# Level scores of a gated recurrence: one product of 128 rows with both heads side by side, or one product of 64 rows for each head

## The chip, the cores and the metric

The kernel is one program on 1 core of a Trainium2 chip. The metric is the device time of an execution in microseconds (us); the time before is a median of 3 runs. Everything is 32-bit float. An f32 product appears in the trace as two records of TensorE work (PE) and two weight loads (PEld); one such record is called a pass here.

## What is computed

One inference step of a backbone of two layers for 1024 latent and 128 context tokens. The change lies in one of the three mixers of a layer, the bidirectional gated linear recurrence with 4 heads of width 64:

```python
def step(state, blk):
    qc, kc, vc, gc = blk
    b = jnp.cumsum(gc, axis=2)
    o_inter = jnp.einsum('nhtk,nhkv->nhtv', qc * jnp.exp(b), state)
    rel = jnp.where(lower, b[:, :, :, None, :] - b[:, :, None, :, :], -jnp.inf)
    att = jnp.einsum('nhtk,nhtsk,nhsk->nhts', qc, jnp.exp(rel), kc)
    o = o_inter + jnp.einsum('nhts,nhsv->nhtv', att, vc)
...
o, s_fin = _gla_chunk_scan(
    jnp.concatenate([q, rev(q)], axis=0),
    jnp.concatenate([k_f, rev(k_b)], axis=0),
    jnp.concatenate([v, rev(v)], axis=0),
    jnp.concatenate([g_f, rev(g_b)], axis=0),
    s0.reshape(2 * B, HG_HEADS, HG_DK, HG_DV))
```

Within a chunk, `att` holds for each query t and each earlier key s the sum over k of q·exp(b_t − b_s)·k. The kernel works on chunks of 128 tokens (NT = 9 of them: 8 latent, 1 context).

## The kernel before

`project_and_recur` is one stage of a layer. On TensorE it does the input projection (`piece()`, 8 products of 128x128 weights each, lines L288 with 256 columns and L291 with 384) and, threaded between the pieces, the recurrence. Two heads share a tile of 128 partitions: head 0 of a pair `ct` lies on partitions 0 to 63, head 1 on 64 to 127.

To avoid overflow in exp(b_t − b_s), the scores are made in levels: at level h a chunk is cut into blocks of 2h tokens, and the queries of one half of each block meet the keys of the other half, with weights relative to the middle of the block. There are 7 levels (h = 64 ... 1) for each of two directions, and two "plain" steps for the diagonal, which take both gates' keys and so twice the products: 16 steps for a pair of heads, NS = 32 steps in a layer, in the order `seq`. Only half of the tokens are queries at a level, 64 of each chunk.

A step n passes three engines:

- VectorE (DVE), in the order `span(n + 2)`, `operands(n + 1)`, `place(n)`. `span` takes two differences (L647, L648). `operands` makes the weighted keys (L665) and the weighted queries in two operations, one for each head's 64 partitions (L668, twice). `place` copies the scores of both heads from PSUM under a mask into `att` (L685).
- ScalarE (ACT): the exponential of the weights (L512), or for a plain step a copy of the queries in two operations (L519). It also empties the pieces' PSUM banks (L433).
- TensorE: `level_scores(n)`. For each chunk the weights are the keys (128 partitions, 128 tokens), and the moving operand is `xq`, 128 partitions by 2 x 64 columns. Head 0's queries stand in the first 64 columns on partitions 0 to 63, head 1's in the last 64 columns on partitions 64 to 127; the rest of `xq` was cleared once by GpSimd (POOL), so that one product gives both heads' scores (L336, 9 products, 18 passes; 36 passes in a plain step).

Scores of even and odd steps lie in two regions of 1536 columns (three PSUM banks of 512) each. A `piece()` follows the scores of 26 of the 32 steps (`with_piece`); steps 3, 7, 11, 19, 23 and 27 are followed directly by the next step's scores. Up to step 9 the pieces are of 384 columns, from step 10 on of 256. After steps 15 and 31 comes `recurrent_out` (L348, L352). After the last step the stage goes on with projection pieces to its end. TensorE's order is written out:

```python
for n in range(NS):
    level_scores(n)
    if n in with_piece:
        piece()
    if n in (NS // 2 - 1, NS - 1):
        recurrent_out(n // (NS // 2))
```

Other lines that come up below: L315 (`state_updates`) are products on 64 columns of the array, L706 the chain of states on DVE ahead of step 0; L812 are the score products of the attention stage, on rows 0 to 63 and 64 to 127 of the array in turn, each pair into two banks; L826 are transposes, L1137 products of 64 rows in the filter stage, and L1201 plain products of 128 rows and 512 columns.

Of the kernel before, what the change touches and what calls it, by code (L numbers as in the profile page):

```python
# [19 lines left out]
ALU = mybir.AluOpType  # L20
ACT = mybir.ActivationFunctionType
AX = mybir.AxisListType

P = 128
# [3 lines left out]
TOK = LAT + CTX  # L28
NT = TOK // P
# [6 lines left out]
DQ = 64  # L36
# [10 lines left out]
LEVELS = [64, 32, 16, 8, 4, 2, 1]  # L47
# [78 lines left out]
def project_and_recur(nc, m, l):  # L126
# [8 lines left out]
                "keys_taken", "decay", "update", "chained", "s_stored", "s_cleared", "mask_loaded", "att_cleared",  # L135
                "span", "cleared", "weight", "operand", "plain", "scores", "placed", "out_done", "out_taken", "g_loaded",
                "step", "root", "out_ready", "hg_turned", "hg_kept")
# [37 lines left out]

    def queries(b, hh, h):
        return m.xq[hh * DQ:(hh + 1) * DQ, b, :, hh].rearrange("p c (b j) -> p c b j", j=h)

# [4 lines left out]
    with stage(nc, m, *HG_NAMES, *PR_NAMES, *AT_NAMES) as (block, s):  # L183
# [72 lines left out]
        @block.gpsimd  # L256
        def _(pool):
            for d in range(2):
                last = nc.gpsimd.memset(m.S[d][:, :, :, :], 0.0)
            last.then_inc(s["s_cleared"], 1)  # L260
            nc.gpsimd.memset(m.xq[:, :, :, :, :], 0.0)
            pool.wait_ge(s["transposed"], 4)
            nc.gpsimd.memset(m.X[:, :, :], 0.0).then_inc(s["cleared"], 1)
            pool.wait_ge(s["update"], len(steps))
            for ct in range(2):
                nc.gpsimd.memset(m.att[:, ct], 0.0).then_inc(s["att_cleared"], 1)
            pool.wait_ge(s["tables_loaded"], 32)
            for i in range(8):
                pool.wait_ge(s["shuffled"], i + 1)
                x = m.aqk[:, i, 0:LAT]  # L270
                nc.gpsimd.tensor_tensor(x, x, m.cos[:, :], ALU.mult).then_inc(s["kept"], 1)

        @block.tensor
        def _(pe):
# [45 lines left out]
            def level_scores(n):  # L320
                ct, d, lev = seq[n]
                if n == 0:
                    pe.wait_ge(s["chained"], 8 * len(steps))
                if n >= 2:
                    pe.wait_ge(s["placed"], n - 1)
                if n == NL + len(LEVELS):
                    pe.wait_ge(s["out_taken"], 3)
                if lev < len(LEVELS):
                    pe.wait_ge(s["operand"], ops[n])
                else:  # L330
                    pe.wait_ge(s["plain"], n + 1 - ops[n])
                operands = [m.X[:, n % 2]] if lev < len(LEVELS) else [m.fk[:, ct], m.fk[:, 2 + ct]]
                for ch in range(NT):
                    at = (n % 2) * 1536 + ch * P
                    for keys in operands:
                        last = nc.tensor.matmul(m.ps[:, at:at + P], keys[:, ch * P:(ch + 1) * P],  # L336
                                                m.xq[:, n % 2, ch].rearrange("p hh t -> p (hh t)"),
                                                start=keys is operands[0], stop=keys is operands[-1])
                last.then_inc(s["scores"], 1)

            def recurrent_out(ct):
                pe.wait_ge(s["placed"], (ct + 1) * (NS // 2))
                for ch in range(NT):
                    at = ch * P
# [5 lines left out]
                    for hh in range(2):  # L350
                        h = 2 * ct + hh
                        last = nc.tensor.matmul(m.ps[:, at + hh * DQ:at + (hh + 1) * DQ], m.att[:, ct, hh, ch, :],  # L352
                                                m.hi[:, ch, h * DQ:(h + 1) * DQ], start=(ch == LT),
                                                stop=(hh == 1 or ch == LT))
# [44 lines left out]
        def _(act):  # L399
# [106 lines left out]
            def weight(n):  # L506
# [7 lines left out]
                else:  # L514

                    act.wait_ge(s["scores"], n - 1)
                    for hh in range(2):
                        r = slice(hh * DQ, (hh + 1) * DQ)
                        last = nc.scalar.activation(  # L519
                            m.xq[r, n % 2, :, hh],  # L520
                            m.hq[r, ct].rearrange("p (c j two) -> p c j two", c=NT, two=2)[:, :, :, lev - len(LEVELS)],
                            ACT.Copy)
                    last.then_inc(s["plain"], 1)

# [42 lines left out]
        def _(dve):  # L567
# [82 lines left out]
            def operands(n):  # L650
# [14 lines left out]
                nc.vector.tensor_tensor(keys, wk, k0, ALU.mult)  # L665
                for hh in range(2):
                    r = slice(hh * DQ, (hh + 1) * DQ)
                    last = nc.vector.tensor_tensor(queries(b, hh, h), wq[r], q0[r], ALU.mult)  # L668
                last.then_inc(s["operand"], 1)

            def place(n):
# [4 lines left out]
                else:  # L676
                    dve.wait_ge(s["placed"], n)
                h = LEVELS[lev] if lev < len(LEVELS) else 1
                dat = m.ps[:, (n % 2) * 1536:(n % 2) * 1536 + TOK]\
                    .rearrange("p (c hh b j) -> p hh c b j", c=NT, hh=2, j=h)  # L680
                msk = m.mask[:, d, lev].rearrange("p (b j) -> p b j", j=h)
# [1711 lines left out]
def build(nc, d, outs):  # L2393
    m = Mem()
# [3 lines left out]
    with ExitStack() as ctx:  # L2398
# [39 lines left out]
        m.E = view(38692, 2, TOK)  # L2438
        m.xq = view(40996, 2, NT, 2, 64)
        m.ke_t = view(43300, NT, 4, P)  # L2440
# [245 lines left out]
```

## Time and profile before

| | us |
|---|---|
| median of 3 runs (lowest, highest) | 4122.88 (4119.47, 4123.29) |
| the profiled execution's own time | 4124.99 |
| its span, first to last instruction | 4123.2 |
| PE busy | 3780.1 (92%) |
| PEld busy (weight loads, beside PE) | 3031.4 (74%) |
| DVE busy | 1624.5 (39%) |
| ACT busy | 1135.8 (28%) |
| POOL busy | 178.3 (4%) |
| mean granted TensorE clock | 0.957 of 2.4 GHz |

Shares are means over the span; the stage in question lies in two stretches, one a layer, with its steps from 332 to 524 us and from 2376 to 2567 us. Ends of matmuls are modelled, and their starts are measured, so distances between starts are the safer reading. A start of a row is where its first instruction starts; the number after it is how long the engine was busy with the row's instructions; in brackets stands the idle time before it and what ended it.

A row of a group by line gives the busy time, the mean duration of one instruction in ns, the idle time of the engine before them and what ended it. A row of a stretch gives its bounds and length, then the busy time and number of instructions of PE, PEld, DVE, ACT and POOL, the granted TensorE clock as a share of 2.4 GHz, the busy share of the DMA engines and GB/s.

### The profile page before, as it was taken

The page shows a single profiled execution, that of the slowest core. Times are in us where ns is not written, and L with a number is a line of the kernel's source. Part 1 is how long each engine was busy: PE and PEld are TensorE (multiplying, and loading weights), DVE is VectorE, ACT ScalarE, POOL GpSimd, SP SyncE. Part 2 cuts the span into 40 slices and gives each one's busy share as a digit, 9 for nine tenths or more (in the row PEclk, how much of TensorE's full clock was granted, in tenths as well). Part 3 has the DMA queues.
Part 4 walks back from the last instruction along what each step waited for, and adds up shares of the span by engine and source line. Part 5 has one row for each costly group of instructions (what it writes and reads, how often), then busy time and mean ns, then how long its engine had stood idle before and what let it go on. Part 6 is the DMA issues. An engine that isn't in the chain of part 4 may idle for free. (4 is left out here: it accounts for less than half of the span.)

```text
span 4123.2 us, 55496 instructions
## 1 busy us (share of the span) xinstructions
PE 3780.1 (92%) x23454; PEld 3031.4 (74%) x23454; DVE 1624.5 (39%) x2890; ACT 1135.8 (28%) x2894; POOL 178.3 (4%) x110
## 2 busy tenths in 40 slices
PE   8899998997949999999889999989879499999996
PEld 3466975666429999999735679656664399999995
DVE  4238723878351111111152487248783511111112
ACT  3442212874111111111145322138721111111112
POOL 0000001000000000000000000110000000000000
PEclk9999999998979999999999999999999699999998
DMA  7411021003246787777582110210122477787784
GB/s 278 149 52 47 29 81 71 1 2 128 96 169 232 279 278 269 269 267 277 175 302 85 48 44 31 86 61 1 67 70 101 157 265 271 280 280 273 272 280 173
DMA packets 319422, 648.97 MB, mean 157 GB/s; under 512 B 19838, under 2 KB 57342, under 8 KB 318408
## 3 DMA queue, kind: packets, MB, share of 16 engines
q1 hardware_dynamic: 305640, 596.14, 39.9%
q0 software_dynamic: 9216, 33.56, 3.5%
q10 hardware_dynamic: 4320, 15.73, 1.0%
q8 instruction: 187, 3.06, 0.3%
q14 instruction: 59, 0.48, 0.0%
HBM read 581.41 MB, written 63.98 MB: 157 GB/s over the span
## 5 line engine op out<-in xcount | busy, mean ns | idle before, releaser
L2149 PE MATMUL ps<-arena 128*128 128x144 f32 x8192 | 1015.4, 287 | 10.3 <-DVE arena L2309 10.3
L2149 PEld LDWEIGHTS ps<-arena 128*128 128x128 f32 x8192 | 1008.5, 190 | 17.9 <-DVE arena L2309 17.9
L291 PE MATMUL ps<-arena 128*128 128x384 f32 x1920 | 629.6, 489 | 2.7 <-PEq L89 2.7
L291 PEld LDWEIGHTS ps<-arena 128*128 128x128 f32 x1920 | 364.7, 191 | 251.1 <-issue 7.2
L2173 PE MATMUL ps<-arena 128*128 128x144 f32 x4096 | 507.1, 286 | 0.0
L2173 PEld LDWEIGHTS ps<-arena 128*128 128x128 f32 x4096 | 503.6, 190 | 0.0
L2320 DVE TENSOR_TENSOR arena<-arena,ps 128x144 f32<-128x144 f32 x256 | 77.9, 304 | 920.6 <-ACT arena L2225 920.6
L2225 ACT ACTIVATE arena<-ps 128x144 f32<-128x144 f32 x256 | 74.5, 291 | 1012.0 <-PE ps L2149 1012.0
L433 ACT ACTIVATE arena<-ps 128x384 f32<-128x384 f32 (+1 forms) x192 | 86.2, 449 | 693.2 <-PE ps L291 462.9
L2309 DVE TENSOR_SCALAR arena<-ps,mod 128x128 f32<-128x128 f32 x256 | 87.1, 403 | 435.5 <-PE ps L2129 435.5
L288 PE MATMUL ps<-arena 128*128 128x256 f32 x1152 | 256.4, 380 | 0.0
L1699 PE MATMUL ps<-arena 128*128 128x512 f32 x576 | 250.4, 593 | 0.0
L943 ACT ACTIVATE arena<-ps,arena 128x512 f32<-128x512 f32 (+2 forms) x400 | 239.6, 615 | 34.5 <-DVE arena L882 33.0
L2232 ACT ACTIVATE arena<-ps,mod 128x128 f32<-128x128 f32 (+1 forms) x512 | 136.5, 318 | 386.2 <-PE ps L2173 386.2
L288 PEld LDWEIGHTS ps<-arena 128*128 128x128 f32 x1152 | 216.8, 191 | 28.5
L880 DVE TENSOR_REDUCE arena<-ps 128x2 f32<-128x1024 f32 (+1 forms) x192 | 189.7, 1041 | 63.5 <-PE ps L812 63.5
L1699 PEld LDWEIGHTS ps<-arena 128*128 128x128 f32 x576 | 108.2, 190 | 132.6 <-issue 132.6
L812 PE MATMUL ps<-arena 64*128 64x512 f32 (+2 forms) x800 | 186.1, 572 | 16.0 <-PEq L89 10.1
L336 PEld LDWEIGHTS ps<-arena 128*128 128x128 f32 x1296 | 158.0, 197 | 28.5 <-issue 22.6
L336 PE MATMUL ps<-arena 128*128 128x128 f32 x1296 | 159.3, 281 | 20.9 <-DVE arena L668 20.0
L846 PE MATMUL ps<-arena 128*128 128x128 f32 x1296 | 161.5, 280 | 4.0 <-ACT arena L962 4.0
L846 PEld LDWEIGHTS ps<-arena 128*128 128x128 f32 x1296 | 154.3, 196 | 5.8 <-ACT arena L954 5.8
(325 smaller groups left out, 3491.8 us busy)
## 6 DMA issues: line engine op xcount, KB each, us to landing
arena<-in_w_gate SPq DMA_DIRECT2D x64, 2048.0 KB, 8.0
arena<-in_w_up SPq DMA_DIRECT2D x64, 2048.0 KB, 14.2
arena<-in_w_down SPq DMA_DIRECT2D x64, 2048.0 KB, 12.4
arena<-in_w_mod SPq DMA_DIRECT2D x24, 2048.0 KB, 15.3
arena<-in_w_in SPq DMA_DIRECT2D x28, 1024.0 KB, 5.1
arena<-in_dft_units SPq DMA_DIRECT2D x26, 512.0 KB, 10.3
arena<-x_rows SPq DMA_DIRECT2D x23, 512.0 KB, 6.1
x_rows<-arena ACTq DMA_DIRECT2D x18, 512.0 KB, 2.6
```

The lines of the kernel that those rows point to most:

```text
L288: last = nc.tensor.matmul(m.ps[:, at:at + 256], m.hT[:, k, q * P:(q + 1) * P], m.Wr[:, slot % 2, k, :], start=(k == 0), stop=(k == KD - 1))
L291: last = nc.tensor.matmul(m.ps[:, at:at + TC], m.Wr[:, slot % 2, k, jj * P:(jj + 1) * P], m.hT[:, k, q * TC:(q + 1) * TC], start=(k == 0), ...
L336: last = nc.tensor.matmul(m.ps[:, at:at + P], keys[:, ch * P:(ch + 1) * P], m.xq[:, n % 2, ch].rearrange("p hh t -> p (hh t)"), start=keys ...
L812: last = nc.tensor.matmul(banks[g][:, mp, 0:keys.shape[1]], m.aqk[r, h, qt * P:(qt + 1) * P], keys[r], start=True, stop=True)
L846: last = nc.tensor.matmul(m.ps[:, 3584:3584 + DV], m.aT[:, n % 2, j, :], v, start=(j == 0), stop=(j == nk - 1))
L880: st.done(nc.vector.tensor_reduce(m.part[:, n % 2, :, g], banks[g], AX.X, ALU.max))
L943: nc.scalar.activation(m.prob[:, n % 2, mp, a:b], banks[g][:, mp, 0:b - a], ACT.Exp, bias=m.nmax[:, n, mp:mp + 1], accum_out=m.sums[:, n, ...
L1699: last = nc.tensor.matmul(m.ps[:, at:at + 512], m.oT[:, k, t * P:(t + 1) * P], m.wo[h][:, k, :], start=(k == 0), stop=(k == KD - 1))
L2149: last = nc.tensor.matmul(m.ps[:, at:at + CAP], m.wbuf[:, 2 * h + which, k, q * P:(q + 1) * P], m.xe[:, e % 2, k, :], start=(k == 0), stop ...
L2173: last = nc.tensor.matmul(m.ps[:, at:at + CAP], m.wbuf[:, 4 + h, k, q * P:(q + 1) * P], m.hid[:, k, :], start=(k == 0), stop=(k == KD - 1))
L2232: last = nc.scalar.activation(m.yT[:, n, a:b], m.ps[:, at + a:at + b], ACT.Copy, scale=m.mod[:, 5 * KD + n, g:g + 1])
L2309: last = nc.vector.tensor_scalar(m.xe[:, e % 2, k, 0:CAP_L], m.ps[:, 3072 + k * P:3072 + (k + 1) * P], m.mod[:, 4 * KD + k, 0:1], m.mod[:, ...
```

## The change

Each head's scores become products of their own, with 64 rows of the array: `score(hh, ch)` takes the keys and the queries on the head's own 64 partitions, 64 columns wide. That is 18 products for a step where there were 9 (36 for 18 in a plain step), in the order head 0, head 1, head 0 and so on. `xq` loses its cleared half and is 64 columns wide for each chunk, so one DVE operation of 128 partitions makes both heads' queries, one ACT operation copies them in a plain step, and POOL no longer clears `xq`. In PSUM head 1's scores stand at columns 0 to 575 of the region and head 0's at 960 to 1535. The first product of head 0 and the last of head 1 lie in the same bank, and a semaphore `shared_bank` keeps the last behind the first. `place` reads that layout and writes `att` with the two heads exchanged; `recurrent_out` reads them exchanged.

```diff
-    def queries(b, hh, h):
-        return m.xq[hh * DQ:(hh + 1) * DQ, b, :, hh].rearrange("p c (b j) -> p c b j", j=h)
+    def queries(b, h):
+        return m.xq[:, b].rearrange("p c (b j) -> p c b j", j=h)
...
-            nc.gpsimd.memset(m.xq[:, :, :, :, :], 0.0)
...
-                for ch in range(NT):
-                    at = (n % 2) * 1536 + ch * P
+                def score(hh, ch):
+                    r, at = slice(hh * DQ, (hh + 1) * DQ), (n % 2) * 1536 + (1 - hh) * 960 + ch * 64
                     for keys in operands:
-                        last = nc.tensor.matmul(m.ps[:, at:at + P], keys[:, ch * P:(ch + 1) * P],
-                                                m.xq[:, n % 2, ch].rearrange("p hh t -> p (hh t)"),
+                        last = nc.tensor.matmul(m.ps[:, at:at + 64], keys[r, ch * P:(ch + 1) * P], m.xq[r, n % 2, ch],
                                                 start=keys is operands[0], stop=keys is operands[-1])
-                last.then_inc(s["scores"], 1)
+                    return last
+
+                score(0, 0).then_inc(s["shared_bank"], 1)
+                for ch in range(1, NT):
+                    score(1, ch - 1)
+                    score(0, ch)
+                pe.wait_ge(s["shared_bank"], n + 1)
+                score(1, NT - 1).then_inc(s["scores"], 1)
...
-                        last = nc.tensor.matmul(m.ps[:, at + hh * DQ:at + (hh + 1) * DQ], m.att[:, ct, hh, ch, :],
+                        last = nc.tensor.matmul(m.ps[:, at + hh * DQ:at + (hh + 1) * DQ], m.att[:, ct, 1 - hh, ch, :],
...
-                    for hh in range(2):
-                        r = slice(hh * DQ, (hh + 1) * DQ)
-                        last = nc.scalar.activation(
-                            m.xq[r, n % 2, :, hh],
-                            m.hq[r, ct].rearrange("p (c j two) -> p c j two", c=NT, two=2)[:, :, :, lev - len(LEVELS)],
-                            ACT.Copy)
-                    last.then_inc(s["plain"], 1)
+                    nc.scalar.activation(
+                        m.xq[:, n % 2],
+                        m.hq[:, ct].rearrange("p (c j two) -> p c j two", c=NT, two=2)[:, :, :, lev - len(LEVELS)],
+                        ACT.Copy).then_inc(s["plain"], 1)
...
-                for hh in range(2):
-                    r = slice(hh * DQ, (hh + 1) * DQ)
-                    last = nc.vector.tensor_tensor(queries(b, hh, h), wq[r], q0[r], ALU.mult)
-                last.then_inc(s["operand"], 1)
+                nc.vector.tensor_tensor(queries(b, h), wq, q0, ALU.mult).then_inc(s["operand"], 1)
...
-                dat = m.ps[:, (n % 2) * 1536:(n % 2) * 1536 + TOK]\
-                    .rearrange("p (c hh b j) -> p hh c b j", c=NT, hh=2, j=h)
+                dat = m.ps[:, (n % 2) * 1536:(n % 2) * 1536 + 1920].rearrange("p (hh x) -> p hh x", hh=2)[:, :, 0:NT * 64]\
+                    .rearrange("p hh (c b j) -> p hh c b j", c=NT, j=h)
...
-        m.xq = view(40996, 2, NT, 2, 64)
+        m.xq = view(40996, 2, NT, 64)
```

## Rows read from the trace of the kernel before

**Rows 1.** Groups by line from 0 to 600 us.

```profile
L336 PE MATMUL ps<-arena 128*128 128x128 f32 x648 | 80.2, 282 | 10.5 <-DVE arena L668 10.0 <-issue 0.5
...
L668 DVE TENSOR_TENSOR arena<-arena 64x576 f32<-64x576 f32 x56 | 42.0, 750 | 0.4
...
L1201 PE MATMUL ps<-arena 128*128 128x512 f32 x64 | 28.8, 592 | 0.0
...
L352 PEld LDWEIGHTS ps<-arena 128*128 128x128 f32 x72 | 9.3, 192 | 0.0
...
L315 PE MATMUL ps<-arena 128*64 128x64 f32 x128 | 4.0, 223 | 0.0
```

**Rows 2.** Timeline of PE, steps 19 to 25 of the first layer.

```profile
454.66 4.18 PE L336 MATMUL ps<-arena 128*128 128x128 f32 x36
458.68 3.62 PE L288 MATMUL ps<-arena 128*128 128x256 f32 x16
462.14 2.17 PE L336 MATMUL ps<-arena 128*128 128x128 f32 x18
...
473.06 2.17 PE L336 MATMUL ps<-arena 128*128 128x128 f32 x18
478.91 3.60 PE L336 MATMUL ps<-arena 128*128 128x128 f32 x18 [3.67 <-DVE arena L668]
...
485.80 2.17 PE L336 MATMUL ps<-arena 128*128 128x128 f32 x18
```

**Rows 3.** Timeline of PE around step 24 of the second layer.

```profile
2515.69 2.17 PE L336 MATMUL ps<-arena 128*128 128x128 f32 x18
2521.51 2.91 PE L336 MATMUL ps<-arena 128*128 128x128 f32 x18 [3.65 <-DVE arena L668]
...
2528.72 0.50 PE L336 MATMUL ps<-arena 128*128 128x128 f32 x3
```

**Rows 4.** Timeline of PE, steps 0 and 1 of the first layer.

```profile
332.31 4.18 PE L336 MATMUL ps<-arena 128*128 128x128 f32 x18 [6.33 <-DVE arena L668]
...
342.49 2.17 PE L336 MATMUL ps<-arena 128*128 128x128 f32 x18
```

**Rows 5.** Timeline of PE, steps 0 to 2 of the second layer.

```profile
2376.34 3.77 PE L336 MATMUL ps<-arena 128*128 128x128 f32 x18 [6.34 <-DVE arena L668]
...
2385.11 2.17 PE L336 MATMUL ps<-arena 128*128 128x128 f32 x18
...
2392.28 2.17 PE L336 MATMUL ps<-arena 128*128 128x128 f32 x18
```

**Rows 6.** Timeline of DVE, steps 19 to 24 of the first layer.

```profile
456.87 1.41 DVE L685 COPY_PREDICATED arena<-arena,ps 128x1152 f32<-128x1152 uint32 x1 [0.67 <-PE ps L336]
...
477.25 1.51 DVE L668 TENSOR_TENSOR arena<-arena 64x576 f32<-64x576 f32 x2
```

**Rows 7.** Timeline of PE, end of the stage and what follows.

```profile
626.07 62.09 PE L291 MATMUL ps<-arena 128*128 128x384 f32 x192
```

**Rows 8.** Timeline of PE in the attention stage, 800 to 812 us.

```profile
802.16 1.99 PE L812 MATMUL ps<-arena 64*128 64x512 f32 x8
```

**Rows 9.** The same at 802.16 to 802.30 us, PE.

```profile
801.96 0.27 PE L826 MATMUL ps<-ident,arena 128*128 128x128 f32 x1
802.16 0.70 PE L812 MATMUL ps<-arena 64*128 64x512 f32 x2
```

**Rows 10.** The same at 802.16 to 802.30 us, weight loads.

```profile
802.16 0.30 PEld L812 LDWEIGHTS ps<-arena 64*128 64x128 f32 x4 [0.17 <-issue]
```

**Rows 11.** Timeline of weight loads in `recurrent_out`, moving operand of 64 columns.

```profile
436.63 0.97 PEld L352 LDWEIGHTS ps<-arena 128*128 128x128 f32 x8
```

**Rows 12.** Timeline of PE at 310.08 to 310.25 us: from 64-column tiles back.

```profile
309.89 0.40 PE L315 MATMUL ps<-arena 128*64 128x64 f32 x8
310.23 0.59 PE L291 MATMUL ps<-arena 128*128 128x384 f32 x1
```

**Rows 13.** A stretch with pairs of 64-row products (L1137) at 38.0 us.

```profile
38.00:41.40 3.40, 1.89 (x8) 0.59 (x8) 2.32 (x3) 0.60 (x1) 0.00 (x0) 1.00 1.04 385
```

More of the change, by code:

```diff
@@ L135, in project_and_recur @@
                 "keys_taken", "decay", "update", "chained", "s_stored", "s_cleared", "mask_loaded", "att_cleared",
-                "span", "cleared", "weight", "operand", "plain", "scores", "placed", "out_done", "out_taken", "g_loaded",
+                "span", "cleared", "weight", "operand", "plain", "shared_bank", "scores", "placed", "out_done", "out_taken", "g_loaded",
                 "step", "root", "out_ready", "hg_turned", "hg_kept")
```

## The prediction, as it was made before the result was known

> **What bounds the kernel now.** I read the groups by line first, for the engines of this stage. The score products (L336, 648 passes a layer) take 80.2 us of PE, and the engine stood idle before them for 10.5 us in all, nearly all of it behind the query multiplications L668 [rows 1]. So the stage hangs on TensorE, and DVE holds it up in few places. The timeline of PE says where. Steps 19 to 23 follow without a gap, 3.67 us are lost ahead of step 24, and in the second layer 3.65 us at the same step [rows 2, 3]. The other idle time stands ahead of step 0, 6.3 us in each layer, while DVE finishes the chain of states and the first operands [rows 4, 5]. After the steps, PE goes on without a gap through the projection to the stage's end: the 192 passes from 626.07 us last 62.09 us [rows 7]. A microsecond that PE gains or loses in the steps is therefore gained or lost in the stage. The chain of waits that ended last covers only the kernel's end and says nothing here.
>
> Each gap costs more than itself, since the clock falls in it: 18 passes behind the first gap last 4.18 us where they last 2.17 otherwise, the lower of the two levels (1.2 instead of 2.4 GHz) [rows 2, 4]. Step 24 to step 25 takes 6.89 us (478.91 to 485.80) where a block of scores and a piece take 2.00 + 3.46 = 5.46. Step 23 to step 24 takes 5.85 where a block of scores takes 2.00. Together that is 1.43 + 3.85 = 5.3 us [rows 2]. In the second layer it is 2521.51 − 2515.69 − 2.00 = 3.8 and 2528.72 − 2521.51 − 5.46 = 1.75, together 5.6 us [rows 3].
>
> **The score block on PE.** Before, the 36 passes of two steps in a row take 4.02 us (454.66 to the next piece at 458.68), so a step takes 2.00 and a pass 0.111; a piece takes 3.46 (458.68 to 462.14) [rows 2]. After, there are 36 passes of 64 columns, 18 on each half of the array. Three questions decide.
>
> Do the halves work at once? L812 is the nearest row: passes of 64 rows and 512 columns, alternating in the same way. Eight of them take 1.99 us [rows 8]. One pass of 512 columns on the whole array takes 28.8 / 64 = 0.45 us [rows 1], so eight in a row would take 3.6. They do run in pairs. The loads do too: four in 0.30 us, where one takes 0.19 and four in a row at this distance would take 0.52 [rows 1, 10, 11].
>
> How long does a pair take? The moving half gets shorter, but the weights keep 128 columns. In `recurrent_out` (L352), where 64 columns move, eight loads take 0.97 us; less the 0.19 of one load that is 0.78 for seven distances, 0.111 each [rows 1, 11]. So 18 pairs have the pace of 18 old passes: 17 x 0.111 + 0.055 for the last stream, 1.94 us against 2.00. The saving is 0.05 us a block, since the old last pass streamed for 0.11.
>
> What does the change of tile cost? The trace shows a delay wherever PE goes over to tiles of another shape: the next load starts late, and that first load is not hidden. Going in: L812 follows L826 by 0.20 us instead of 0.11, and its first pass lasts 0.70 where L1201, of 512 columns too, lasts 0.59; 0.09 + 0.11 = 0.20 [rows 1, 9]. Coming out: the last L315 starts at 310.07 (309.89 + 0.40 less the 0.22 of one), L291 at 310.23, 0.16 later, less 0.055 for the stream; and that first L291 lasts 0.59, at 384 columns as long as L1201 with 128 more, which stream for 0.45 / 4 = 0.11. That is 0.10 + 0.11, 0.20 again [rows 1, 12].
>
> The Trainium skill says both things. "TensorEngine Tiling (Array Packing)", Key Properties: a change of tiling mode, not of tile, drains the engine; the trace agrees, with 0.20 us each way. "TensorE: Matmul & The Clock Gate", LDWEIGHTS: a load's time goes by its columns and not by its rows. The trace agrees here as well, 0.111 for 128 columns.
>
> A block thus costs 0.20 − 0.05 + 0.20 = 0.35 us more, whether of one step, of two in a row or of a plain step, since the length falls out. A layer has 26 blocks (32 steps, 6 of them joined to the one before): 26 x 0.35 = 9.1. Steps 0 and 16 come after idle time, in which the emptying is hidden: less 2 x 0.2. That leaves 8.7 a layer, **17.4 us more**. The wait on `shared_bank` costs nothing: its product is the first of the block, done 1.5 us before the last one is due, and 16 products are queued ahead of the waiting one. If the queue were stopped by it, about 0.1 us a step would be added, 6 us in all.
>
> **DVE.** Two operations L668 become one of 128 partitions. An operation of 64 partitions and 576 elements takes 0.75 us (42.0 / 56) [rows 1], so one of them, 0.75 us, goes from each level step. Is that enough for step 24? Count from T, the start of step 19's scores, 454.66. The new PE needs 4.02 + 0.35 for steps 19 and 20, then three pieces of 3.46, two blocks of 2.35, and for step 23 an entry of 0.20 and 2.00: it asks for step 24 at T + 21.65. DVE starts place(19) at 456.87, T + 2.21, and ends the queries of step 24 at 477.25 + 1.51, 21.9 us later [rows 6]. After: T + 2.4 (entry), + 21.9, less 4 x 0.75, plus 0.1 for the semaphore and 0.1 for a wait on scores in between: T + 21.5. The stall is gone, with 0.15 us to spare, and with it the slow clock: **10.9 us less**. The cover is thin, but what would be left is a few tenths, too short to look like the gaps above.
>
> Step 0 needs its operands one operation earlier: 0.75 us in each layer, **1.5 us less**. In the other steps PE never waited, and DVE, which becomes faster while PE becomes slower, has more room than before, so the copies L685 may take their other PSUM layout at the old price, or at 0.1 us more, for nothing. The same holds for the one ACT copy less in plain steps, and POOL's clearing lies ahead of all this, off the path.
>
> **Step 0 at the slow clock.** Steps 0 to 1 take 10.18 us in the first layer and 8.77 in the second, where steps 1 to 2 take 7.17 (2392.28 − 2385.11) [rows 4, 5]: 3.0 and 1.6 us are paid until the clock is back. In the new block each half streams only 0.055 of every 0.111 us, and the clock may rise later. The two layers differ by 1.4 us; I take half of it each, **1.4 us more**, between 0 and 2.8.
>
> **Sum:** 17.4 − 10.9 − 1.5 + 1.4 = +6.4 us. The profiled execution took 4125.0 and would take 4131.4; it lay 2.1 above the median, so the median goes from 4122.9 to 4129.3.
>
> **Rivals.** (a) *The changes of tile cost little here.* The 0.20 rests on other shapes, and part of it could overlap with the queue's work. At nothing, the blocks give 26 x 0.05 x 2 = 2.6 us, and the sum is −2.6 − 12.4 + 0 to 1.4: about 4108, faster. It decides from 0.2 us a block instead of 0.4 on. Against it: three kinds of transition in the trace show the same.
>
> (b) *The block becomes half as long*, if loads of half the rows were half as long. It would save 1.0 us per 18 passes, 36 such units a layer, 72 us: about 4057. The two pairs of loads in 0.30 us speak against it: a pair waits 0.11 for the one before [rows 10]. The Trainium skill, "TensorEngine Tiling (Array Packing)", Theoretical Speedup, gives up to 2x for a dimension of 64; only the first of these prices would make it true here.
>
> (c) *The clock falls inside the blocks*, slower. The array is half used for 4.3 us in the 6 joined and 4 plain blocks of a layer. A fall cost 1.4 to 3.0 us behind the gaps above; ten a layer would add 28 to 60 us, to 4157 to 4189, and one in three some 15, to 4145. It shows from two falls on. Against it: in a stretch of pairs of 64-row products, PE busy 1.89 of 3.40 us, the granted clock stayed 1.00 [rows 13].
>
> (d) *The halves don't overlap*, for instance through the shared bank or the order: 18 x 0.111 = 2.0 us more per unit, 72 x 2.0 = 144 us: about 4273. The eight passes in 1.99 us speak against it [rows 8].
>
> **Chances.** My forecast 0.67, (a) 0.11, (b) 0.02, (c) 0.13, (d) 0.04, another way 0.03. The likeliest case's own range is 4122 to 4138: 6 us for the queue stopped by the wait, ± 1.4 for step 0, up to 3 for changes of tile that cost 0.17 or 0.23, a remnant of the stall at step 24. To hold 8 in 10 the range takes in part of (a) and the lower part of (c): 4112 to 4146. Within 0.2% (8.2 us, 4114.6 to 4131.1), about what a measurement can tell from no change, lie six tenths of my case and little of the others: 0.45. Above it lie the rest of my case, (c) and (d): 0.41. Below lie (a), (b) and a part of the unnamed: 0.14.
>
> **What would show it.** The groups should show L336's successors with 1296 passes of 64x128 with 64 columns a layer, a block that lasts 1.95 us from first to last start at a pace of 0.111, and a piece that starts 0.15 us after the last start; step 1 to 2 takes 7.5 us instead of 7.17. DVE has one operation of 128x576 in L668's place, and no idle time stands ahead of step 24. I am wrong if the pace of a pair is not 0.111, if the first piece after a block comes without delay, if a wait on DVE remains, or if the granted clock drops between 340 and 520 us.

## The result, and the profile after

| | before | after |
|---|---|---|
| median (lowest, highest) of 11 runs each, us | 4124.25 (4119.47, 4127.45) | 4132.82 (4127.68, 4135.15) |
| ratio of times, 95% interval | | 1.0022 (1.0014 to 1.0030) |
| the profiled execution's own time | 4124.99 | 4127.68 |
| its span | 4123.2 | 4125.9 |

The change makes the kernel 8.6 us slower by the medians, 0.2%; 6.4 were forecast. The profiled execution of after was the fastest of its 11 and lies only 2.7 us above that of before. So the stage is read by itself: from the first of the `state_updates` (L315 before, L314 after) to the first product of the attention stage it takes 392.5 us in the first layer and 393.2 in the second (before 389.3 and 388.2), together 8.2 us more. The work between the two stages, which no kernel of this study changes, took 1654.7 us in the profile of before and 1650.7 in that of after, and between 1649.2 and 1656.3 in all thirteen profiles: whole executions differ by that much without any cause in the stage.

Of all executions in this study one, of the kernel with queries on GpSimd, was in a second, slower state (4311.1 us at a mean granted clock of 0.888, where its five others took 4096.0 to 4100.1 at 0.959 to 0.962); it counts in that kernel's median, which would be 4097.8 without it, and not in its ratio.

The groups by line from 0 to 600 us, after. In this kernel L335 are the score products, L649 and L650 the differences of `span`, L667 the keys, L668 the queries, L684 the copy under a mask, L287 and L290 the pieces of 256 and 384 columns:

```profile
L335 PE MATMUL ps<-arena 64*128 64x64 f32 x1296 | 80.0, 278 | 6.0 <-DVE arena L668 5.6 <-issue 0.5
...
L684 DVE COPY_PREDICATED arena<-arena,ps 128x1152 f32<-128x1152 uint32 x32 | 61.3, 1915 | 65.3 <-PE ps L335 65.3
```

Beside [rows 1]: twice as many passes, in pairs, busy as long as before (80.0 us for 80.2). The wait behind the queries falls from 10.0 to 5.6 us, and what is left is step 0 alone. But busy time does not hold the loss: while the engine goes over to another tile there is no idle time in this column. The starts show it. PE, steps 19 to 25 of the first layer, after:

```profile
461.65 4.24 PE L335 MATMUL ps<-arena 64*128 64x64 f32 x72
465.81 3.72 PE L287 MATMUL ps<-arena 128*128 128x256 f32 x16
469.46 2.23 PE L335 MATMUL ps<-arena 64*128 64x64 f32 x36
471.62 3.72 PE L287 MATMUL ps<-arena 128*128 128x256 f32 x16
475.27 2.23 PE L335 MATMUL ps<-arena 64*128 64x64 f32 x36
477.43 3.72 PE L287 MATMUL ps<-arena 128*128 128x256 f32 x16
481.08 4.24 PE L335 MATMUL ps<-arena 64*128 64x64 f32 x72
```

Beside [rows 2]: step and piece take 5.81 us (469.46 to 475.27) where they took 5.46; the joined steps 19 and 20 with their piece take 7.81 (461.65 to 469.46), not 7.48. Both are 0.34 more, whatever the block's length. The piece is busy for 3.72 us instead of 3.62, its first load being visible. The stall ahead of step 24 is gone: the 72 passes of steps 23 and 24 go through.

The last two passes of such a block, one on each half, after:

```profile
471.41 0.28 PE L335 MATMUL ps<-arena 64*128 64x64 f32 x2
```

The piece behind them starts at 471.62, 0.20 us after the last pass.

DVE at that place, after:

```profile
477.54 2.75 DVE L684 COPY_PREDICATED arena<-arena,ps 128x1152 f32<-128x1152 uint32 x1 [0.39 <-PE ps L335]
480.08 0.79 DVE L649 TENSOR_TENSOR arena<-arena 128x576 f32<-128x576 f32 x1
480.78 0.75 DVE L650 TENSOR_TENSOR arena<-arena 128x576 f32<-128x576 f32 x1
481.44 0.77 DVE L667 TENSOR_TENSOR arena<-arena 128x576 f32<-128x576 f32 x1
482.11 0.76 DVE L668 TENSOR_TENSOR arena<-arena 128x576 f32<-128x576 f32 x1
483.35 1.49 DVE L684 COPY_PREDICATED arena<-arena,ps 128x1152 f32<-128x1152 uint32 x1 [0.48 <-PE ps L335]
```

One L668 of 0.76 us stands where two took 1.51 [rows 6]. The queries of step 24 end at 482.87, 0.26 us ahead of that step's first start at 483.13 (the 37th of the 72 passes). DVE now waits for PE where it was behind. The copies take as long as before.

Step 0 in the two layers, after:

```profile
333.49 4.11 PE L335 MATMUL ps<-arena 64*128 64x64 f32 x36 [5.57 <-DVE arena L668]
337.52 6.95 PE L290 MATMUL ps<-arena 128*128 128x384 f32 x16
344.41 2.23 PE L335 MATMUL ps<-arena 64*128 64x64 f32 x36
```

```profile
2376.69 4.11 PE L335 MATMUL ps<-arena 64*128 64x64 f32 x36 [5.57 <-DVE arena L668]
2380.72 7.64 PE L290 MATMUL ps<-arena 128*128 128x384 f32 x16
2388.29 2.23 PE L335 MATMUL ps<-arena 64*128 64x64 f32 x36
```

The wait is 0.76 us shorter in each [rows 4, 5]. The time from step 0 to 1 is 10.92 and 11.61 us where 7.51 is the rate at the full clock, so 3.4 and 4.1 us go to the slow clock (3.0 and 1.6 before). In the second layer the piece now takes 7.64 us. Before, it ran at the full clock:

```profile
2379.95 5.33 PE L291 MATMUL ps<-arena 128*128 128x384 f32 x16
```

From 340 to 520 us the mean granted clock is 1.00, and the same from 2390 to 2570 us, which answers rival (c) for this kernel. The stretch of the first layer, after:

```profile
340.00:520.00 180.00, 179.55 (x1645) 147.84 (x1644) 121.30 (x131) 41.80 (x56) 0.00 (x0) 1.00 0.12 40
```

### The profile page after: what moved, and what is told of

Read it like the earlier page. It is cut to its first block and busy times, and to the rows that moved or that the text cites. A ratio compares the mean times of both kernels' runs of the same rounds, so it can differ in the third digit from the quotient of the medians.

```text
span 4125.9 us, 58022 instructions
## 1 busy us (share of the span) xinstructions
PE 3795.8 (92%) x24750; PEld 3031.3 (73%) x24750; DVE 1581.8 (38%) x2834; ACT 1129.5 (27%) x2886; POOL 174.4 (4%) x108
## 5 line engine op out<-in xcount | busy, mean ns | idle before, releaser
L2148 PEld LDWEIGHTS ps<-arena 128*128 128x128 f32 x8192 | 1008.4, 190 | 17.9 <-DVE arena L2308 17.9
L290 PE MATMUL ps<-arena 128*128 128x384 f32 x1920 | 632.2, 490 | 2.5 <-PEq L89 2.5
L290 PEld LDWEIGHTS ps<-arena 128*128 128x128 f32 x1920 | 365.0, 191 | 252.7 <-issue 8.2
L2172 PEld LDWEIGHTS ps<-arena 128*128 128x128 f32 x4096 | 503.6, 190 | 0.0
L287 PE MATMUL ps<-arena 128*128 128x256 f32 x1152 | 259.0, 382 | 0.0
L287 PEld LDWEIGHTS ps<-arena 128*128 128x128 f32 x1152 | 215.8, 190 | 30.7
L1698 PEld LDWEIGHTS ps<-arena 128*128 128x128 f32 x576 | 108.2, 190 | 132.6 <-issue 132.6
L335 PEld LDWEIGHTS ps<-arena 64*128 64x128 f32 x2592 | 152.9, 191 | 32.8 <-issue 30.1
L684 DVE COPY_PREDICATED arena<-arena,ps 128x1152 f32<-128x1152 uint32 x64 | 122.8, 1918 | 131.3 <-PE ps L335 131.3
L335 PE MATMUL ps<-arena 64*128 64x64 f32 x2592 | 160.1, 278 | 12.1 <-DVE arena L668 11.1
L845 PE MATMUL ps<-arena 128*128 128x128 f32 x1296 | 159.8, 278 | 4.0 <-ACT arena L961 4.0
```

Of the source, the lines that this page charges most:

```text
L287: last = nc.tensor.matmul(m.ps[:, at:at + 256], m.hT[:, k, q * P:(q + 1) * P], m.Wr[:, slot % 2, k, :], start=(k == 0), stop=(k == KD - 1))
L290: last = nc.tensor.matmul(m.ps[:, at:at + TC], m.Wr[:, slot % 2, k, jj * P:(jj + 1) * P], m.hT[:, k, q * TC:(q + 1) * TC], start=(k == 0), ...
L335: last = nc.tensor.matmul(m.ps[:, at:at + 64], keys[r, ch * P:(ch + 1) * P], m.xq[r, n % 2, ch], start=keys is operands[0], stop=keys is o ...
L684: nc.vector.copy_predicated(out, msk, dat).then_inc(s["placed"], 1)
L845: last = nc.tensor.matmul(m.ps[:, 3584:3584 + DV], m.aT[:, n % 2, j, :], v, start=(j == 0), stop=(j == nk - 1))
L1698: last = nc.tensor.matmul(m.ps[:, at:at + 512], m.oT[:, k, t * P:(t + 1) * P], m.wo[h][:, k, :], start=(k == 0), stop=(k == KD - 1))
```

## The experiments

Ratios are against the kernel before, run on the same chip in the same rounds, with 95% intervals.

**The change without the one query operation.**

```diff
-                nc.vector.tensor_tensor(queries(b, h), wq, q0, ALU.mult).then_inc(s["operand"], 1)
+                for hh in range(2):
+                    r = slice(hh * DQ, (hh + 1) * DQ)
+                    last = nc.vector.tensor_tensor(queries(b, h)[r], wq[r], q0[r], ALU.mult)
+                last.then_inc(s["operand"], 1)
```

> The changed kernel, but the queries of a level step are again made by two operations of 64 partitions. If the one operation is what removed the stall ahead of step 24, DVE comes 4 x 0.75 = 3.0 us later there, and PE, which had 0.15 us to spare, waits about 2.9 us in each layer and then runs some 1.4 us at the slow clock; step 0 comes 0.75 us later: about 10 us more than the changed kernel, 18 more than before. Rival: the stall vanished because PE itself became slower (0.35 us a block). Then no wait comes back, only step 0 is later, and the time is 1.5 us above the changed kernel's.

Measured: 4146.7 us, ratio 1.0056 (1.0040 to 1.0073), some 14 us above the changed kernel. PE around step 24:

```profile
480.37 2.23 PE L335 MATMUL ps<-arena 64*128 64x64 f32 x36
485.22 3.10 PE L335 MATMUL ps<-arena 64*128 64x64 f32 x36 [2.63 <-DVE arena L670]
488.25 6.14 PE L287 MATMUL ps<-arena 128*128 128x256 f32 x16
494.32 2.23 PE L335 MATMUL ps<-arena 64*128 64x64 f32 x36
```

The stall is back, 2.63 us in each layer. The rival falls: a PE slower by 0.35 us a block does not remove it alone. The slow clock behind it costs more than expected: step 24 with its piece takes 9.10 us (485.22 to 494.32) and not 5.81, 3.3 us instead of 1.4; from step 23 to step 25 it is 13.96 us for the 7.82 of the changed kernel. The clock falls about 1 us into the block, after the wait is over, and stays low through the rest of it and most of the piece:

```profile
485.20:486.20 1.00, 0.98 (x18) 1.00 (x19) 1.00 (x1) 0.00 (x0) 0.00 (x0) 1.00 0.00 0
486.20:488.20 2.00, 2.00 (x23) 1.94 (x20) 2.00 (x4) 0.26 (x1) 0.00 (x0) 0.54 0.00 0
488.20:491.00 2.80, 2.80 (x9) 2.21 (x8) 2.75 (x4) 0.90 (x1) 0.00 (x0) 0.50 0.00 0
```

**The one operation without the change on PE.**

```diff
-                for hh in range(2):
-                    r = slice(hh * DQ, (hh + 1) * DQ)
-                    last = nc.vector.tensor_tensor(queries(b, hh, h), wq[r], q0[r], ALU.mult)
-                last.then_inc(s["operand"], 1)
+                nc.vector.tensor_tensor(m.xq[:, b, :, 0].rearrange("p c (b j) -> p c b j", j=h), wq, q0,
+                                        ALU.mult).then_inc(s["operand"], 1)
```

> The kernel before with its products of 128 rows, but one query operation of 128 partitions, which writes head 1's queries into head 0's columns: head 1's scores are left out and head 0's are mixed with them, the work on PE is as before. This is the DVE part of the change alone. Theory: the stall ahead of step 24 goes (10.9 us with its slow clock) and step 0 comes earlier (1.5 us): 12.4 us less than before, a ratio of 0.997. DVE then needs T + 21.5 and PE asks at T + 20.4 (no slower blocks), so a remnant of about 1 us a layer may stay: 10 us less. Rival: the queries' time is hidden anyway and PE's slower blocks removed the stall: within 2 us of before.

Measured: 4109.0 us, ratio 0.9967 (0.9953 to 0.9982), 13.6 us less. The stall at step 24 is 0.25 us, and no slow clock follows it:

```profile
470.62 2.17 PE L336 MATMUL ps<-arena 128*128 128x128 f32 x18
473.05 2.25 PE L336 MATMUL ps<-arena 128*128 128x128 f32 x18 [0.25 <-DVE arena L666]
475.13 3.62 PE L288 MATMUL ps<-arena 128*128 128x256 f32 x16
```

So the DVE part alone is worth all of its 12 us; the stage takes 383.0 and 382.8 us, 11.7 less than before in the two layers. What the change adds on PE costs more than that: from this kernel to the changed one the two stages grow by 19.9 us.

**One change of tile in each block, and no more products.**

```diff
+                    r = slice(0, P if ch < NT - 1 else DQ)
                     for keys in operands:
-                        last = nc.tensor.matmul(m.ps[:, at:at + P], keys[:, ch * P:(ch + 1) * P],
-                                                m.xq[:, n % 2, ch].rearrange("p hh t -> p (hh t)"),
+                        last = nc.tensor.matmul(m.ps[:, at:at + P], keys[r, ch * P:(ch + 1) * P],
+                                                m.xq[r, n % 2, ch].rearrange("p hh t -> p (hh t)"),
```

> The kernel before, but the last chunk's product of each step takes 64 rows of the array instead of 128 (head 1's scores of that chunk are left out). The number of products is as before, and each block goes over to another tile shape and back once. Theory (the change of tile costs 0.20 us each way): each block of a step becomes 0.40 us longer, 32 blocks of a step a layer since joined steps now change tile too, about 0.4 x 32 x 2 = 25 us more on PE, of which some 4 x 0.4 us a layer only fill the stall ahead of step 24 and are not paid: about 22 us more than before. Rival (the loss of the changed kernel comes from the doubled number of products, not from the change of tile): within 2 us of before.

Measured: 4142.1 us, ratio 1.0044 (1.0028 to 1.0061), 19.5 us more than before, with the number of passes unchanged:

```profile
463.55 4.76 PE L337 MATMUL ps<-arena 128*128 128x128 f32 x36
468.24 3.72 PE L288 MATMUL ps<-arena 128*128 128x256 f32 x16
471.79 2.36 PE L337 MATMUL ps<-arena 128*128 128x128 f32 x18
474.08 3.72 PE L288 MATMUL ps<-arena 128*128 128x256 f32 x16
477.64 2.36 PE L337 MATMUL ps<-arena 128*128 128x128 f32 x18
```

Step and piece take 5.85 us (471.79 to 477.64), 0.39 more than 5.46. The joined steps 19 and 20 change tile twice as often, and take 8.24 with their piece (463.55 to 471.79), 0.76 more than 7.48. The loss thus goes by the number of changes and not by the number of products. The slower PE fills part of the stall at step 24: it is 2.11 us in the first layer where it was 3.67, the 4 x 0.4 us that were expected.

**Half of the moving columns.**

```diff
-                        last = nc.tensor.matmul(m.ps[:, at:at + 64], keys[r, ch * P:(ch + 1) * P], m.xq[r, n % 2, ch],
+                        last = nc.tensor.matmul(m.ps[:, at:at + 32], keys[r, ch * P:(ch + 1) * P], m.xq[r, n % 2, ch, 0:32],
```

> The changed kernel, but only 32 of the 64 query columns move through the array (half of the scores are left out). Theory: the weight loads set the pace, 0.111 us a pair of passes whatever moves, so that a block lasts 1.95 us from its first start to its last as in the changed kernel, and the time is the same but for 0.03 us a block, 2 us. Rival: the moving columns set the pace; a block then takes about half, 1.0 us, and the time is 72 us lower.

Measured, one run: 4160.6 us, 28 above the changed kernel, which neither theory gives. The trace holds two findings. PE, steps 7 to 9, and the stretches around them:

```profile
379.72 3.39 PE L290 MATMUL ps<-arena 128*128 128x384 f32 x10
383.04 4.21 PE L335 MATMUL ps<-arena 64*128 64x32 f32 x72
387.18 7.12 PE L290 MATMUL ps<-arena 128*128 128x384 f32 x16
```

```profile
340.00:520.00 180.00, 179.54 (x1538) 146.11 (x1536) 116.26 (x128) 40.45 (x54) 0.00 (x0) 0.93 0.12 39
388.00:396.00 8.00, 8.00 (x47) 4.96 (x45) 5.41 (x8) 2.71 (x3) 0.00 (x0) 0.81 0.00 0
```

First, 72 passes of 32 columns keep the pace of 72 passes of 64: 4.21 us instead of 4.24. The moving columns do not set it, and the rival is out; what is the same in both, and in the old passes of 128 rows and columns with their 0.111 us, is the load of 128 weight columns. Second, the granted clock now falls at joined and plain blocks: over the 180 us it is 0.93 where it was 1.00, though PE was idle for no more than 0.46 us of them (0.45 in the changed kernel), and the piece behind steps 7 and 8 takes 7.12 us instead of 5.43. Such a loss comes seven times in each layer, at joined and plain blocks or just behind them, 1.6 to 3.3 us each against the changed kernel. This is rival (c), one step further than the change went. The single run is no accident of its execution: the two stages take 406.7 and 406.9 us, 27.9 more than in the changed kernel, and the work between them 1654.7 us, as before.

**Both heads on the same half.**

```diff
-                    r, at = slice(hh * DQ, (hh + 1) * DQ), (n % 2) * 1536 + (1 - hh) * 960 + ch * 64
+                    r, at = slice(0, DQ), (n % 2) * 1536 + (1 - hh) * 960 + ch * 64
```

> The changed kernel, but both heads' products take rows 0 to 63 (head 1's scores are left out, head 0's are made twice). Theory: what keeps the changed kernel near the old one is that the two halves work at once. Without it the 36 passes of a step follow one another at 0.111 us: 4.0 us a block instead of 1.95, 36 x 2.0 x 2 = 144 us more, about 4277. Rival: passes of 64 rows and 64 columns on one half are not bound by loads and take 0.055 each, and the time stays.

Measured, one run: 4434.4 us, 302 above the changed kernel. PE in steps 2 and 3, the group of the score products, and the stretch:

```profile
349.54 4.23 PE L335 MATMUL ps<-arena 64*128 64x64 f32 x36
353.70 7.12 PE L290 MATMUL ps<-arena 128*128 128x384 f32 x16
```

```profile
L335 PE MATMUL ps<-arena 64*128 64x64 f32 x1296 | 189.1, 316 | 6.0 <-DVE arena L668 5.6 <-issue 0.5
```

```profile
340.00:520.00 180.00, 180.00 (x861) 145.71 (x861) 67.25 (x72) 21.34 (x29) 0.00 (x0) 0.74 0.08 26
```

At the full clock 36 passes in a row on one half take 4.23 us, and 2.23 in the changed kernel, so the halves do work at once there and that is worth the 144 us of rival (d). The other half of the loss, some 158 us, is again the clock, 0.74 in this stretch, in which PE was never idle. Here too the two stages agree (541.6 and 543.4 us), and the work between them takes 1656.1 us.

**Steps joined in twos**, in the changed kernel. Pieces stand behind odd steps only:

```diff
-    with_piece = [n for n in range(NS) if n % 4 != 3 or n in (15, 31)]
+    with_piece = [16 * half + n for half in range(2) for n in (1, 1, 3, 5, 5, 7, 7, 9, 9, 11, 11, 13, 15)]
...
-                if n in with_piece:
+                for _ in range(with_piece.count(n)):
                     piece()
```

> The changed kernel with its steps joined in twos: pieces stand only behind odd steps, one or two each, 26 a layer as before. Blocks fall from 26 to 16 a layer. Theory (each block pays for its two changes of tile and not for its length): 10 x 0.34 x 2 = 6.8 us less than the changed kernel, as long as DVE still delivers in time (it has some 11 us for two steps and needs 8 to 11). Rival: the extra time lies in the passes, so joining saves nothing, or DVE is late at one block a layer and each wait costs 2 us or more.

Measured: 4125.4 us, ratio 1.0006 (0.9996 to 1.0015). By the ratios that is 6.6 us less than the changed kernel, with about 5 either way. The traces of these two show less: steps 0 to 31 take 188.3 and 188.0 us, in the changed kernel 188.5 and 189.2. Joining steps 0 and 1 puts two blocks into the slow clock, and there are waits of 0.38 us on DVE at step 21 and ahead of `recurrent_out`. The saving is there but in part spent again; how much stays open within that interval.

**One piece moved**, in the kernel before.

```diff
-    with_piece = [n for n in range(NS) if n % 4 != 3 or n in (15, 31)]
+    with_piece = [n for n in range(NS) if n % 4 != 3 or n in (15, 23, 31)]
+    with_piece.remove(30)
```

> The kernel before with one projection piece moved in each layer: from behind step 30, where DVE waits, to behind step 23, where PE waited 3.67 us for the queries. Nothing else is changed. Theory: the piece of 3.46 us fills the stall, so the stall and the slow clock after it go without any change of the products: 10.9 us less than before, less than 1 us left. Rival: DVE is late at the next step instead, or the joined steps 30 and 31 wait: less than half of that gain.

Measured: 4111.3 us, ratio 0.9972 (0.9962 to 0.9982), 11.8 less. Around steps 24 and 28:

```profile
476.51 2.25 PE L337 MATMUL ps<-arena 128*128 128x128 f32 x18 [0.20 <-DVE arena L669]
...
496.01 2.25 PE L337 MATMUL ps<-arena 128*128 128x128 f32 x18 [0.86 <-DVE arena L669]
```

The stall of 3.67 us becomes 0.20 and 0.86, both without a slow clock. The order of one piece gives what the DVE part of the change gave.

**The pieces placed anew, in both kernels.** One more stands ahead of step 0. In the kernel before one also goes behind step 23, and those behind 14 and 30 go; in the changed kernel the one behind 30 goes. The lines that both have in common:

```diff
-    AT_LEVELS = FIRST_HY + 10
+    AT_LEVELS = FIRST_HY + 11
...
-            for _ in range(3):
+            for _ in range(4):
                 piece()
```

> The kernel before with its products and operations as they were and the pieces placed anew: one piece more ahead of step 0, where PE waited 6.3 us in each layer, one behind step 23, none behind steps 14 and 30. Theory: the wait at step 0 shrinks by a piece of 384 columns (5.2 us) and the slow clock after it (3.0 and 1.6 us) goes, the stall at step 24 goes with its clock (5.3 and 5.6): about 26 us less than before, 4098. Rival: the clock still falls in the rest of the first wait, or DVE becomes late between steps 11 and 16: 11 to 18 us less.

> The changed kernel with one piece more ahead of step 0 and none behind step 30. Theory: its wait at step 0 is 5.57 us and falls to 0.4, and the slow clock behind it goes, 3.4 us in the first and 4.1 us in the second layer: 17.9 us less than the changed kernel, about 9 us less than before. It stays some 10 to 17 us above the kernel before with its pieces placed anew (4104.7 where it was measured), since the 26 blocks a layer keep their changes of tile. Rival: with both waits filled the two forms meet within 4 us.

Measured: before with its pieces placed anew 4104.7 us, ratio 0.9958 (0.9944 to 0.9971); the changed kernel with them 4110.2 us, ratio 0.9966 (0.9953 to 0.9978). Step 0, first the one, then the other:

```profile
330.96 2.25 PE L338 MATMUL ps<-arena 128*128 128x128 f32 x18 [1.18 <-DVE arena L670]
333.04 5.33 PE L293 MATMUL ps<-arena 128*128 128x384 f32 x16
```

```profile
331.16 2.23 PE L336 MATMUL ps<-arena 64*128 64x64 f32 x36 [0.42 <-DVE arena L669]
333.31 5.43 PE L291 MATMUL ps<-arena 128*128 128x384 f32 x16
```

At step 0 most of the wait is gone in both, and the slow clock with it. In the kernel before that is 18.4 us less, at the upper end of the rival's 11 to 18, where 26 were forecast. The changed kernel now lies 15.3 us below before; against itself it gains 18.6 us in the two stages (17.9 forecast). The two forms come closer than the 10 to 17 us forecast: by their own times they are 5.5 apart, by their ratios 3. In the traces the stage takes 379.2 us in each layer in the one and 383.5 and 383.6 in the other, 4.4 a layer and not 8. With PE's long waits filled, the old form is the one that DVE holds up: 1.18 us at step 0, 0.86 at step 28, 0.2 at step 24, and 1.44 us behind the copy L687 ahead of `recurrent_out` after step 15, while the changed form waits 0.42 us at step 0 and pays its changes of tile.

**Products of 128 rows, head 1's queries on GpSimd**, with one piece more ahead of step 0 and none behind step 30.

```diff
+            for n, (ct, d, lev) in enumerate(seq):
+                if lev < len(LEVELS):
+                    b, h, r = n % 2, LEVELS[lev], slice(DQ, P)
...
+                    wq, q0 = halves(m.E[:, b, 0:TOK], h)[1 - d], halves(m.hq[:, ct], h)[1 - d]
+                    nc.gpsimd.tensor_tensor(queries(b, 1, h), wq[r], q0[r], ALU.mult).then_inc(s["operand1"], 1)
...
-                for hh in range(2):
-                    r = slice(hh * DQ, (hh + 1) * DQ)
-                    last = nc.vector.tensor_tensor(queries(b, hh, h), wq[r], q0[r], ALU.mult)
-                last.then_inc(s["operand"], 1)
+                r = slice(0, DQ)
+                nc.vector.tensor_tensor(queries(b, 0, h), wq[r], q0[r], ALU.mult).then_inc(s["operand"], 1)
```

> The kernel before with its products of 128 rows and one piece more ahead of step 0 (none behind step 30); head 1's query operation goes from DVE to GpSimd, which is idle there, so that DVE has its 0.75 us a step without any change of tile. GpSimd took 3.39 us for 1024 columns, so some 1.9 us for 576 are estimated. Theory: as the changed kernel with its pieces placed anew, but without 8.7 us a layer for changes of tile: 4110.2 - 17.4 = 4093. Rival: GpSimd's later queries or its sharing of memory ports with DVE make PE wait again; then the time is no lower than that of the kernel before with its pieces placed anew, 4105 or more.

Measured: 4098.4 us, ratio 0.9935 (0.9923 to 0.9948), the fastest of the study and 25 us below before. The groups between 320 and 520 us:

```profile
L347 PE MATMUL ps<-arena 128*128 128x128 f32 x648 | 76.8, 275 | 1.7 <-issue 1.7
...
L276 POOL TENSOR_TENSOR arena<-arena 64x576 f32<-64x576 f32 x26 | 38.8, 1493 | 135.0 <-PE ps L347 94.4 <-ACT arena L523 40.5
...
L659 DVE TENSOR_TENSOR arena<-arena 128x576 f32<-128x576 f32 x26 | 22.0, 844 | 0.0
```

GpSimd takes 1.49 us for an operation that DVE does in 0.75. It works mostly beside the copy under a mask and reaches into the DVE operation behind that (L659, the L647 of before), which takes 0.84 us instead of 0.76 on average. By the whole trace 30 of its 56 overlap GpSimd and take 0.90 on average, up to 1.12; the others take 0.77. So the rival is there, but small. PE waits 1.7 us ahead of the score products of the first layer where it waited 10.5. Of the 17 us that were to come on top of the changed kernel with its pieces placed anew, 12 came.

**The same pieces and steps joined in twos, in the changed kernel.**

```diff
-    with_piece = [n for n in range(NS) if n % 4 != 3 or n in (15, 31)]
+    with_piece = [16 * half + n for half in range(2) for n in (1, 1, 3, 5, 5, 7, 7, 9, 9, 11, 11, 13, 15)]
+    with_piece.remove(27)
...
-    AT_LEVELS = FIRST_HY + 10
+    AT_LEVELS = FIRST_HY + 11
```

> The changed kernel with one piece more ahead of step 0 and its steps joined in twos, 16 blocks a layer instead of 25. Theory: 9 blocks fewer save 9 x 0.34 x 2 = 6 us: 4104. Rival: the first two steps now stand together and DVE is late for the second, and DVE waits come elsewhere: no gain over 4110.

Measured: 4109.2 us, ratio 0.9963 (0.9950 to 0.9976): no difference from 4110.2 that can be told. Steps 0 to 31 take 178.4 us instead of 179.6, a third of the 3.1 a layer that nine fewer blocks should give. Step 1 now waits 0.48 us for DVE, `recurrent_out` 0.39 and step 21 0.38, together 1.25 of the 1.9 us that are missing. Steps 0 and 1:

```profile
332.39 2.23 PE L336 MATMUL ps<-arena 64*128 64x64 f32 x36 [0.42 <-DVE arena L669]
335.10 2.23 PE L336 MATMUL ps<-arena 64*128 64x64 f32 x36 [0.48 <-DVE arena L669]
```

## Why the prediction held, step by step

**The pace of a block** was right: 36 passes in pairs take 1.95 us from first to last start, and half the columns do not change it (4.21 for 4.24 us); one half alone takes nearly twice as long.

**The changes of tile** were right: 0.34 us a block for 0.35. The intervals between the steps of a layer, without step 0 and steps 23 and 24, add up to 7.85 us more; with those blocks' own share (0.34 and 0.35) and 0.29 behind step 31 that is 8.8 a layer, where 8.7 were forecast. Only the sum of the two ways was right, 0.39 us for 0.40, and that was luck in part. Going in costs 0.14: the block starts 0.09 late, as forecast, but its first pair is only 0.05 longer (its passes last 0.32 instead of 0.27), where a load of 0.11 was to be seen. Coming out costs 0.25: the piece starts 0.20 us after the last pass, where 0.15 was named as the sign, and its first pass is 0.10 longer. The experiment with one product of 64 rows a block shows the cause without the doubled products. The wait on `shared_bank` cost nothing that can be seen: the last pair, which stands behind it, starts 0.11 us after the one before it, like all the others.

**The stall at step 24** was right in size (from step 23 to 25 4.9 and 5.2 us less, with 0.35 of new cost inside them, so 5.3 and 5.6) and in cause: without the one operation it comes back with 2.63 us (2.9 expected), and with that operation alone it is 0.25. One reading behind it was loose: the clock need not fall in the wait. In the kernel with two query operations it fell only in the block behind it, as the rows there show.

**Step 0 at the slow clock** was mis-sized. I took 1.4 us for both layers, with 0 to 2.8 as its bounds, and the trace shows (10.92 − 10.18 − 0.34) + (11.61 − 8.77 − 0.34) = 2.9. It is the one term that was off, and it was a guess: half of the difference between two layers. Other runs bear the measured size out. The slow clock cost 3.1 to 3.5 us a layer in the two other kernels with the new block at step 0 behind such a wait (two query operations; half the columns), and 1.5 to 2.3 in the three with the old block or nearly it (one operation; one half product; one piece moved). That the half-streaming blocks themselves hold the clock back is the likeliest reading of this, but no run isolates it. The sum with 2.9 is 17.4 − 10.8 − 1.5 + 2.9 = 8.0 us, against 8.6 by the medians and 8.2 in the stages.

**The rivals.** (a) is out: the two changes of tile cost 0.39 us together for these shapes. (b) is out: a load of 64 rows takes 0.188 us and one of 128 rows took 0.192. (d) is out. (c) did not happen here, but with 32 columns it did, at 28 us, the lower end of its price of 28 to 60, and on one half alone it cost some 158. So the changed kernel was nearer to it than the trace of before let one see: the row held against it [rows 13] shows eight passes of 512 columns in 3.4 us, and says nothing of 36 or 72 short ones in a row.

## What to carry to other kernels

Cutting a product into halves of the array saves nothing when the loads of the weights set the pace (here 0.111 us for 128 columns of them), and each excursion to another tile shape costs 0.34 us here however long it is: count the excursions, not the passes. When one edit touches two engines, price them apart. Here the DVE half gained 12 us and the PE half lost 20, and the gain was to be had by itself, by moving one piece of other work into the wait or by giving one operation to an idle engine. A wait on TensorE behind which the clock is low costs more than itself (3.67 us cost 5.3; 2.63 cost 6.1 in the kernel with two query operations), while waits of 0.25 and 0.86 us cost 0.5 and 1.1. So the long ones are the first thing to fill.

## What the runs showed that was not expected

- The granted clock fell without any wait of PE just before. With 32 moving columns a pass the mean over 180 us of blocks and pieces, all but uninterrupted, was 0.93, with 64 on one half 0.74, with 64 on both halves 1.00.
- With the new blocks about 1.5 us more were lost to the slow clock behind the wait at step 0 than with the old ones, and behind the stall at step 24, in the kernel with two query operations, 3.3 us where the old kernel lost 1.4 and 1.75.
- GpSimd multiplied 64 x 576 elements in 1.49 us, less than the 1.9 estimated from its 3.39 us for 1024 columns of 128 partitions, and lengthened the DVE operation behind the copy from 0.77 to 0.90 us where the two overlapped.
